# Dilated attention with its memory work under the projections and its groups combined between memory units; the first modulation mostly on VectorE

## The reference

```
cond = silu(c)
mod = cond @ w_mod[i] + b_mod[i]          # 1024 -> 3072, for each of the first four layers
shift, scale, gate = split(mod, 3)
h = rms_norm(x, norm_pre_g[i]) * (1 + scale) + shift

# dilated attention: 12 heads of 64, three groups of 4 heads with strides 1, 4, 16
for g in range(3):
    logits = q_g @ k_g.T / 8 + bias, within a band
    m = max(logits); p = exp(logits - m); den = sum(p)
    o_g = (p @ v_g) / den;  lse_g = m + log(den)
w = softmax(lse over the three groups)    # for each row and head of a group
mixed = concat(o_g * w_g)                 # 512 x 768
# memory attention: 256 rows mem, 4 heads of 64
k_m, v_m = split(rms_norm(mem) @ w_kv, 2)
o_m = softmax(q_m @ k_m.T) @ v_m          # 512 x 256
out = concat(mixed, o_m) @ w_out
```

## Time and profile before

| | us |
|---|---|
| median of three timed runs | 3152.48 (3150.43 to 3152.56) |
| the profiled execution | 3174.25 |
| its span, first to last instruction | 3172.4 |
| TensorE busy | 2928.9 |
| VectorE busy | 1398.3 |
| ScalarE busy | 1112.3 |
| GpSimd busy | 243.7 |

### The profile page before, as it was taken

The page is one execution under the profiler, slowest core; times in us unless marked ns, Lnnn a source line. Parts: engine busy times, 40 slices in busy tenths (PEclk is TensorE's granted clock), DMA queues, the critical chain, the costliest instruction groups (busy, mean ns, idle before and its releaser), DMA issues. The chain is left out here.

```text
span 3172.4 us, 34865 instructions
## 1 busy us (share of the span) xinstructions
PE 2928.9 (92%) x13946; PEld 2341.5 (74%) x13946; DVE 1398.3 (44%) x2303; ACT 1112.3 (35%) x1951; POOL 243.7 (8%) x400
## 2 busy tenths in 40 slices
PE   8989999999999989998988999999798878899999
PEld 8667777786456768797546888888648878788887
DVE  0576566553444655522135433247532343353332
ACT  1454432423233455423333222142333443242221
POOL 2233021020000022000000000000000000000000
PEclk9999999999569999998558999999867988899999
DMA  4422273463001311322001333333200000033332
GB/s 177 160 81 67 93 244 121 129 201 100 14 24 48 127 53 34 109 80 80 0 1 60 94 99 96 97 102 96 77 0 1 1 1 1 27 93 94 99 93 80
DMA packets 147321, 250.26 MB, mean 79 GB/s; under 512 B 15519, under 2 KB 68026, under 8 KB 146137
## 3 DMA queue, kind: packets, MB, share of 16 engines
q1 hardware_dynamic: 130096, 198.08, 20.0%
q0 software_dynamic: 14816, 48.31, 4.6%
q10 hardware_dynamic: 2249, 1.65, 0.2%
HBM read 245.84 MB, written 5.30 MB: 79 GB/s over the span
## 5 line engine op out<-in xcount | busy, mean ns | idle before, releaser
L209 DVE TENSOR_TENSOR w_lo<-w_raw,w_hi 128x1024 fp32r<-128x1024 f32 (+1 forms) x348 | 413.0, 1193 | 797.5 <-ACT w_hi L202 796.4
L202 ACT ACTIVATE w_hi<-w_raw 128x1024 fp32r<-128x1024 f32 (+1 forms) x348 | 357.7, 1035 | 1109.3 <-DMA w_raw<-in_ffn_w_gate_up 307.7
L217 PE MATMUL PS<-hT_hi,w_hi 128*128 128x512 f32 (+1 forms) x1728 | 659.7, 382 | 20.4 <-DVE hT_lo L797 12.2
L218 PE MATMUL PS<-hT_lo,w_hi 128*128 128x512 f32 (+1 forms) x1728 | 652.9, 378 | 0.0
L219 PE MATMUL PS<-hT_hi,w_lo 128*128 128x512 f32 (+1 forms) x1728 | 652.8, 378 | 0.0
L217 PEld LDWEIGHTS PS<-hT_hi,w_hi 128*128 128x128 f32 x1728 | 331.1, 192 | 82.1 <-issue 15.8
L219 PEld LDWEIGHTS PS<-hT_hi,w_lo 128*128 128x128 f32 x1728 | 331.4, 192 | 58.9
L218 PEld LDWEIGHTS PS<-hT_lo,w_hi 128*128 128x128 f32 x1728 | 331.3, 192 | 57.0 <-issue 0.2
L217 PE MATMUL PS<-w_hi,hT_hi 128*128 128x512 f32 (+1 forms) x736 | 298.0, 405 | 37.4 <-DVE hT_lo L2512 9.1
L218 PE MATMUL PS<-w_lo,hT_hi 128*128 128x512 f32 (+1 forms) x736 | 289.1, 393 | 0.0
L219 PE MATMUL PS<-w_hi,hT_lo 128*128 128x512 f32 (+1 forms) x736 | 288.5, 392 | 0.0
(11 more groups left out here) (530 smaller groups left out, 3916.5 us busy)
## 6 DMA issues: line engine op xcount, KB each, us to landing
w_raw<-in_ffn_w_gate_up SPq DMA_DIRECT2D x176, 256.0 KB, 3.1
mraw<-in_w_mod POOLq DMA_DIRECT2D x160, 256.0 KB, 4.0
w_raw<-in_gla_w_in SPq DMA_DIRECT2D x48, 512.0 KB, 4.3
w_raw<-in_ffn_w_down SPq DMA_DIRECT2D x44, 512.0 KB, 3.7
w_raw<-in_fox_w_in SPq DMA_DIRECT2D x32, 512.0 KB, 4.3
w_raw<-in_sgu_w_in SPq DMA_DIRECT2D x24, 512.0 KB, 4.9
w_raw<-in_dn_w_in SPq DMA_DIRECT2D x24, 512.0 KB, 3.6
w_raw<-in_gla_w_out SPq DMA_DIRECT2D x16, 512.0 KB, 4.5
```

Source lines behind the costliest of these rows:

```text
L202: nc.scalar.activation(w_hi[:, n % NS, :, 0:m], w_raw[:, n % NS, :, 0:m], ACT.Copy).then_inc(w_hidone, 1)
L209: nc.vector.tensor_tensor(w_lo[:, n % NS, :, 0:m], w_raw[:, n % NS, :, 0:m], w_hi[:, n % NS, :, 0:m].bitcast(F32), ALU.subtract).then_inc( ...
L217: nc.tensor.matmul(o, l_hi, r_hi, start=start, stop=False)
L218: nc.tensor.matmul(o, l_hi, r_lo, start=False, stop=False)
```

## The change

**First modulation.** POOL sets the accumulator `macc` to zero before the bias row lands in its first partition. After the four row normalisations DVE adds row tiles 0 to 6 times cond into it, each in one instruction over 2048 columns. TensorE turns the first two row tiles, multiplies row tile 7 as before, and adds 16 products of the accumulator's tiles with a column of ones, which sum over partitions. Cond is computed on ACT after the row squares.

**Gated linear attention, first layer.** The 24 pieces move to levels 1, 2, 3, 5, 7 and to the end of each head; POOL's loads move with them.

**Dilated attention.** The blocks' order is now: three of queries and keys, the memory projection, memory queries, three of values. The memory's transposes stand between the two halves of the second block, with its normalisation on ACT and DVE beside them. The two runs of units become one of 64, and the combination is placed between its memory units on 128 partitions: TensorE brings maxima and sums of the strided groups into row order by four products (`natural_order`), DVE picks and computes [128, 4, 12] weights (`lowest`, `weights`), TensorE spreads them over 64 partitions by 8 products for each pair of heads (`weight_rows`), and DVE multiplies and splits one pair in every second memory unit (`gate`). The output projection waits for the split pairs of rows it needs, not for all.

```diff
         def pool_setup():
             pool = nc.gpsimd
+            pool.memset(macc[:, 0:2 * D], 0.0).then_inc(macc_zero, 1)
+            pool.wait_ge(macc_zero, 1)
...
+        M0 = KT - 1
+
+        def dve_mod_first():
+
+            v = nc.vector
+            v.wait_ge(m_row, mod_rows(0))
+            v.wait_ge(cond_done, 1)
+            for k in range(M0):
+                if k % 2 == 0:
+                    v.wait_ge(m0_landed[k // 2], 16)
+                v.scalar_tensor_tensor(out=macc[:, 0:4 * BW], in0=first_mod[k // 2][:, k % 2, :], scalar=cond[:, k:k + 1],
+                                       in1=macc[:, 0:4 * BW], op0=ALU.mult, op1=ALU.add).then_inc(m0_used, 1)
+                v.wait_ge(m0_used, k + 1)
+
+        def pe_mod_first(bank):
 
             t_ = nc.tensor
-            if ks[0] == 0:
-                t_.wait_ge(cond_done, 1)
-                t_.wait_ge(m_row, mod_rows(0))
-                for j in range(2 * KT):
-                    t_.matmul(PS[:, bank, 2 * j:2 * j + 1], macc[0:1, j * P:(j + 1) * P], ones[0:1, 0:1], start=j == 0, stop=False)
-            for k in ks:
-                if k % 2 == 0:
-                    t_.wait_ge(m0_landed[k // 2], 16)
-                for j in range(2 * KT):
-                    mm = t_.matmul(PS[:, bank, 2 * j:2 * j + 1], first_mod[k // 2][:, k % 2, j * P:(j + 1) * P],
-                                   cond[:, k:k + 1], start=False, stop=k == KT - 1 and j == 2 * KT - 1)
-            if ks[-1] == KT - 1:
-                mm.then_inc(mfin, 1)
+            t_.wait_ge(cond_done, 1)
+            t_.wait_ge(m0_landed[M0 // 2], 16)
+            for j in range(2 * KT):
+                t_.matmul(PS[:, bank, 2 * j:2 * j + 1], first_mod[M0 // 2][:, M0 % 2, j * P:(j + 1) * P], cond[:, M0:M0 + 1],
+                          start=j == 0, stop=False)
+            t_.wait_ge(m0_used, M0)
+            for j in range(2 * KT):
+                mm = t_.matmul(PS[:, bank, 2 * j:2 * j + 1], macc[:, j * P:(j + 1) * P], ones[:, 0:1],
+                               start=False, stop=j == 2 * KT - 1)
+            mm.then_inc(mfin, 1)
...
-                pe_mod_first(7, range(0, 4))
                 for t in range(2):
                     turn(t)
-                pe_mod_first(7, range(4, KT))
+                pe_mod_first(7)
...
                     xsquares(t)
+                act_setup()
...
                     normed(t)
+                dve_mod_first()
                 dve_modfin(0, (7,))
...
-                            if h:
-                                mod_loads(p, i + 1, 27 + 6 * h, 28 + 6 * h)
...
-                        if l >= 3:
-                            mod_loads(p, i + 1, 28 + 6 * h + l - 3, 28 + 6 * h + l - 2)
+                        if l in (3, 4, 5, 7):
+                            s = 28 + 6 * h + (3, 4, 5, 7).index(l)
+                            mod_loads(p, i + 1, s, s + 1)
+                        elif h and l < 3:
+                            mod_loads(p, i + 1, 25 + 6 * h + l, 26 + 6 * h + l)
...
-                        if l < 7:
-                            dve_mod(i + 1, 24 + 6 * h + l - 1, 24 + 6 * h + l)
+                        if l in (1, 2, 3, 5, 7):
+                            s = 24 + 6 * h + (1, 2, 3, 5, 7).index(l)
+                            dve_mod(i + 1, s, s + 1)
...
+                    dve_mod(i + 1, 29 + 6 * h, 30 + 6 * h)
...
+                    if u == 1 and late:
+                        t_.wait_ge(*late)
...
+            r.pick = hf[:, 0, 0:256].rearrange("p (a t) -> p a t", t=TT)
+            r.A = hf[:, 0, 256:352].rearrange("p (t c h) -> p t c h", t=TT, c=2)
+            r.Ex = hf[:, 0, 352:400].rearrange("p (t h) -> p t h", t=TT)
+            r.low = hf[:, 0, 400:416].rearrange("p (t h) -> p t h", t=TT)
...
-            wb = [add_block(w, [(0, 0, BW)], halves=True)] + project(w, [BW, 2 * BW]) + \
-                 [add_block(w, [(0, 3 * BW + 256 * c, 256)]) for c in range(4)]
+            qk0 = add_block(w, [(0, 0, BW)], halves=True)
+            qk1, qk2 = project(w, [BW, 2 * BW])
             kv = add_block(io["mem_w_kv_2"][0], [(0, 0, BW)])
+            qm, v0, v1, v2 = (add_block(w, [(0, 3 * BW + 256 * c, 256)]) for c in (3, 0, 1, 2))
+            wb = [qk0, qk1, qk2, kv, qm, v0, v1, v2]
...
+                part(qk1, T_forms(qk1), 0, 2)
+                pre_pe(mq, [(ps_evac, qk0.ev)], 2, halves_of)
+                part(qk1, T_forms(qk1), 2, 4)
+                t_.wait_ge(mem_x.hf, KT)
+                part(qk2, T_forms(qk2), 0, 4)
                 s = bank_set(kv)
-                t_.wait_ge(mem_x.hf, KT)
                 pe_block(kv, [("T", s, 0), ("T", s + 1, P), ("tok", s + 2, NAT, 0, 256, 256), ("tok", s + 3, NAT, 1, 256, 256)],
                          r.mhi, r.mlo, [(mem_x.split, CK * c + CK) for c in range(KT // CK)])
-                main.pe([(ps_evac, kv.ev), (q.toe, 16 * AH)])
-                mem.pe([(q.ready, 2)])
-
+                pe_block(qm, [("T", bank_set(qm) + j, j * P) for j in range(2)], hT_hi, hT_lo)
+                for g, b in enumerate((v0, v1, v2)):
+                    pe_block(b, [("tok", bank_set(b) + t, ORDER[g], t, 0, 256) for t in range(TT)], hT_hi, hT_lo)
+
+                def natural_order():
+                    for t in range(TT):
+                        mm = t_.matmul(PS[:, 7, 64 * t:64 * t + 64], hf[:, 1, t * P:(t + 1) * P], r.nd[:, :, AHG:AH, :], start=True, stop=True)
+                    mm.then_inc(q.rt, 1)
+
+                def weight_rows(n):
+                    if n == 0:
+                        t_.wait_ge(q.wg, 1)
+                    else:
+                        t_.wait_ge(q.wb, n)
+                    for c in range(2):
+                        for t in range(TT):
+                            mm = t_.matmul(PS[64 * c:64 * c + 64, 7, t * P:(t + 1) * P],
+                                           r.W[:, t, 2 * n + c:2 * n + c + 1].to_broadcast([P, 64]), ident[:], start=True, stop=True)
+                    mm.then_inc(q.wrow, 1)
+
+                def between(u):
+                    if u == NU + 1:
+                        natural_order()
+                    if u >= NU + 4 and u % 2 == 0 and u < NU + 16:
+                        weight_rows((u - NU - 4) // 2)
+
+                t_.wait_ge(q.ready, 2)
+                soft.pe([(ps_evac, v1.ev), (q.toe, 16 * AH)], (ps_evac, v2.ev), between)
                 t_.wait_ge(su.po, AH // 2 + 2)
-                for g in range(3):
-                    for c, a in ((0, r.nm), (1, r.den)):
-                        for t in range(TT):
-                            mm = t_.transpose(PS[0:AHG, 3 * c + g, t * P:(t + 1) * P], a[:, g * AHG:(g + 1) * AHG, t], ident[:])
-                mm.then_inc(q.rt, 1)
-                t_.wait_ge(q.wg, 1)
-                for n in range(AH // 2):
-                    if n >= 2:
-                        t_.wait_ge(q.wb, n - 1)
-                    for e in range(2):
-                        sel = ident[0:AHG, 2 * (n % 2) + e:2 * (n % 2) + e + 1].to_broadcast([AHG, 64])
-                        mm = t_.matmul(PS[64 * e:64 * e + 64, 6 + n % 2, :], sel, Re[:, n // 2, :], start=True, stop=True)
-                    mm.then_inc(q.wrow, 1)
-                t_.wait_ge(q.os, os_at + KT)
+                t_.wait_ge(q.wb, AH // 2)
...
+                pre_act_rows(mq, lambda t: (mem_x.landed, 16), mem_raw, 2)
+                act_feed(ahead(qk1) - 2)
+                pre_act_cols(mq, vcol("mem_norm"), 2, halves_of)
+                block_done(qk1)
...
+                def lowest():
+                    v.wait_ge(q.rt, 1)
+                    then_dve(v.tensor_tensor(r.pick, PS[:, 7, 0:256].rearrange("p (a t) -> p a t", t=TT),
+                                             r.own[:].unsqueeze(1).to_broadcast([P, 64, TT]), ALU.mult))
+                    v.tensor_reduce(out=r.A.rearrange("p t c h -> p (t c) h")[:, :, AHG:AH],
+                                    in_=r.pick.rearrange("p (a h) t -> p a h t", h=2 * AHG), op=ALU.add, axis=AX)
+                    for c in range(2):
+                        ins = v.tensor_copy(r.A[:, :, c, 0:AHG], r.nd[:, c, 0:AHG, :].rearrange("p h t -> p t h"))
+                    then_dve(ins)
+                    then_dve(v.tensor_tensor(r.low, r.A[:, :, 0, 0:AHG], r.A[:, :, 0, AHG:2 * AHG], ALU.min))
+                    then_dve(v.tensor_tensor(r.low, r.low, r.A[:, :, 0, 2 * AHG:AH], ALU.min))
+                    for g in range(3):
+                        gs = slice(g * AHG, g * AHG + AHG)
+                        ins = v.tensor_tensor(r.Ex[:, :, gs], r.A[:, :, 0, gs], r.low, ALU.subtract)
+                    ins.then_inc(q.e1, 1)
+
+                def weights():
+                    v.wait_ge(q.e2, 1)
+                    then_dve(v.tensor_tensor(r.W[:], r.Ex, r.A[:, :, 1, :], ALU.mult))
+                    then_dve(v.tensor_tensor(r.low, r.W[:, :, 0:AHG], r.W[:, :, AHG:2 * AHG], ALU.add))
```

(21 more changed lines are left out.)

162 lines of the change are left out of this document (81 added, 81 removed).

## The result

The changed kernel takes 3062.28 us (median of 4 runs, 3059.28 to 3077.26), the kernel before 3151.45 beside it (4 runs, 3142.61 to 3152.56): ratio 0.9733, 95% interval 0.9695 to 0.977. The forecast was 3069. The profiled executions differ by more than the medians: 3174.25 before, 3065.02 now, 109.2 us. Where the extra 20 are from is the main question of the experiments.

A forecast was written before the change was run, and what follows sets the result against it. TensorE, busy 92% of 3172.4 us, was taken as the bound overall, with cheap or idle stretches. Terms -34.8 - 1 - 17.1 - 28.8 - 2 = -83.7 took the median 3152.5 to 3069 us, range 3010 to 3118.

The forecast's parts named there:

- the carrying over to the median: Whole kernel: sum taken off the profiled 3174.25 us, and the same 21.8 us difference to the median kept, giving 3069.
- First modulation: Kernel start: seven of eight row tiles move to VectorE, so TensorE ends at 44.9 instead of 79.7 us, -34.8.
- Gated layer: First gated layer: the same 24 accumulations and loads at other levels, -1 us, range -4 to +2.3.
- its bound of 6.4: First gated layer: all modulation work there costs at most 101.3 - 94.9 = 6.4 us over four heads.
- Memory work: Dilated attention: memory normalisation, transposes and projection placed under the projections, -17.1 us, bounds -12 and -19.
- Combination: Dilated attention: combination moved between memory units, weight rows lifting the clock there, 50.7 us against 79.5, -28.8.
- own 45 us: Dilated attention, low-clock rival: the memory units' own work never lifts the clock; total 3094 us, chance 0.23.
- work on all 128 rows: Dilated attention's memory units: the first lot of weight rows, products on 128 rows, lifts the clock; the rest keeps it.
- Output projection: After the dilated attention's units: first ten products take 0.23 instead of 0.43 us each at the raised clock, -2.
- The rival of the forgetting attention: Its clock rises at another moment, up to 45 us either way: late about 3114, early 3024; chance 0.16, half late.
- the forecast's own sign: Forgetting attention: the forecast would be wrong if this took other than 170 us.

The follow-up runs named there:

- the same head: Five added dense products behind the first unit's scores of the forgetting attention: on the changed kernel 3051.05 us, on the kernel before 3139.01 us.

## Why the prediction was right

The terms of the sum held; the carrying over to the median held for a reason the forecast did not have. By its own steps:

- **First modulation, -34.8.** Measured -34.7 in the profile, 34.4 in the medians with it undone. Start at 19.14 for 18.3, seven instructions of 2.35 to 2.38 for 2.37. The growth of 0.54 us for every 512 elements, taken from the earlier trace rows, holds up to 2048.
- **Gated layer, -1.** Between -0.1 and -2.8, below what the medians can tell. The 101.3 and 94.9 us that the forecast read as four heads are three, from the end of the first to the end of the last; its bound of 6.4 is one for three heads.
- **Memory work, -17.1.** From the layer's first transposes to the first probability transpose it was 185.6 us (1314.8 to 1500.38) and is 167.0 (1257.8 to 1424.79): -18.6, inside the bounds; 16.5 with it undone. From the last projection product to the first probability transpose it is 3.5 us (1421.32 to 1424.79), where about 3 was expected.
- **Combination, -28.8.** From there to the output projection 184.3 us before and 152.3 now: -32.0. The course was as forecast: the clock low through the 48 units and the first memory units, up in the first lot of weight rows, and the run with the lots behind the units shows that having them between is what brings it up there. Two readings behind it do not hold. The units' "own 45 us" do lift it, at their end (1648.4, the 0.53 of the earlier trace rows), and the reason given, work on all 128 rows, is not shown: with such a product in every short unit the clock fell. Two sizes were off and partly cancel. The five later lots take 1.5 us, not 2.1, and the first 2.4, not 4.2: 4.6 us less. VectorE's scaling holds TensorE five times 0.57 and once 1.48 us, 4.3 in all, where 1.5 was reserved, and that for other operations. From the end of the 48 units the stretch is 47.1 us against 50.7 forecast; 1.8 of these 3.6 are the two sizes, the other 1.8 lie in the units and were not taken apart.
- **Output projection, -2.** Measured -2.2 (38.0 and 35.8 us to the next layer's first transposes).

The sum was -83.7; with the forgetting attention levelled by the same head in both kernels, -88.0 was measured, and the 4.3 us between are mostly the combination's 3.2 and the memory work's 1.5. The medians without heads lie 89.2 us apart. The forecast of the profiled time, 3090.5, was 25.5 us off (3065.02), and those are the 25.9 of the forgetting attention. The forecast carried the 21.8 us between the profiled execution and the median over to the changed kernel without asking where they lie; there they are 2.7. The median still came out at 3062 for 3069, since, as far as the runs with the head show, that layer's long loop was in the profiled execution before and hardly in the medians. That part was luck.

The rival of the forgetting attention did occur in the profiles: the layer gained 25.9 us in the first pair, and by the forecast's own sign (170 us there or it is wrong) this counts against it. But no run shows it to be a result of the change. With its code untouched the loop took 165.8 us in the kernel before, and with the changed kernel and its variants 160.2, 160.2, 137.6, 137.5 (four profiles) and 131.9. The kernel before has only one such profile, so how often it takes the long way is not known. The prediction named it as a moment that depends on something outside the loop; what that is was not found. The change moves it by 35 us, and the profile with these 35 us taken back kept the short loop, while two with the changed start had a long one: the moment alone does not decide it. The medians contain little of it: the dense head brings 11 us to the changed kernel and 12.4 to 17.7 to the one before (3151.45 or 3156.74 against 3139.01).

The rule of the Trainium skill (TensorE: Matmul & The Clock Gate, "Why this matters for your kernels"), by which a TensorE kept busy has the full clock, is not borne out here: 105.2 us without idle time at 0.50, and a head of dense work that hands the clock over to the strided units is lost again 8 to 12 us into them (four profiles) with no idle time between.

## What to carry to other kernels

Read the granted clock for each stretch before costing anything in it: TensorE was busy for all of 105.2 us of small products here at half the clock, and six lots of dense products between such units made the layer 15.8 us shorter than the same lots behind them, because the clock rose for what followed. How much dense work it takes has to be tried: one product more in every unit only cost time. Price a moved step by the nearest row of its own kind and its growth with size, and reserve the wait for the partner engine once for each turn, not once in all. Where a layer that the change does not touch differs between two profiles, level it in both kernels before putting the difference down to the change.

## What the runs showed of the hardware

- Five fp32 products of 512 columns on 128 rows, behind the first scores of a loop that begins at the low clock, lift it: in the four profiles with them they take 5.8 to 7.3 us, and the low stretch is recorded as 23.9 or 27.3 us, where the same code without them has anything from 48 to 126. In the 120 us of the loop behind them it did not fall again.
- With such a head ahead of the dilated attention's units the clock stayed up through 16 units of 256 to 384 columns, and fell 8 to 12 us into units of 128 columns (four profiles), with TensorE busy 100% in both. The runs do not separate the width from what else differs between these units.
- After memory units at 0.50 the clock rose at their end, when transposes and values followed one another without score products: at 1648.4 in the kernel before and at 1597.8 in the run with the weight rows behind the units.
- A score product of 128 columns, whose queries and keys are both read at a stride of four elements, took 0.83 us at either clock, beside 0.33 and 0.47 for a transpose of the same size. In the forgetting attention the same size without a stride takes 0.48 us at the full clock (834.51) and 0.79 at the low one (824.24).
